# Block-diagonal inverse in an RWKV-7 scan: levels up to 32 on 64x64 blocks in four array positions, the mask applied to the first product

## What is computed

```python
def step(S, inp):                        # one head, state S is 64 x 64
    r_t, w_t, k_t, v_t, a_t, b_t = inp
    sa = jnp.einsum('bhij,bhj->bhi', S, a_t)
    S = (S * w_t[:, :, None, :]
         + sa[..., None] * b_t[:, :, None, :]
         + v_t[..., None] * k_t[:, :, None, :])
    y = jnp.einsum('bhij,bhj->bhi', S, r_t)
    return S, y
...
_, y = lax.scan(step, S0, xs)            # 512 steps, 16 heads
```

## Time and profile before

| | |
|---|---|
| median of 3 runs | 3165.78 us (3161.58 to 3166.35) |
| profiled execution | 3160.55 us, of which the span is 3158.7 us |
| PE busy over the span | 97% |
| DVE, ACT, POOL busy | 63%, 40%, 25% |
| the eight groups of the scan | 243.7 to 629.4 us from the span's start |

### The profile page before, as it was taken

One profiled execution on the slowest core, in us unless ns is written; L12 is line 12 of the kernel. 1 busy time (PEld: TensorE's weight loads), 2 busy tenths in 40 slices (PEclk: granted clock), 3 DMA queues, 4 the chain that ended last, 5 costly groups with the idle time before them and its releaser, 6 DMA issues.

```text
span 3158.7 us, 43525 instructions
## 1 busy us (share of the span) xinstructions
PE 3058.2 (97%) x17249; PEld 2662.7 (84%) x17249; DVE 1998.6 (63%) x3594; ACT 1266.9 (40%) x2141; POOL 776.0 (25%) x515
## 2 busy tenths in 40 slices
PE   8999999989999999999999999999999999999999
PEld 6778888878888888888877778999999998888887
DVE  5586665663232464333357755988978877787878
ACT  6364443343232334232234632435445453333432
POOL 1000110100000020000002200686776754343432
PEclk9999999999999999999999999999999999999999
DMA  4313221233333323333232022588889899999997
GB/s 123 111 31 101 62 74 57 72 119 94 100 94 100 114 94 92 95 97 97 87 91 74 1 68 81 185 270 299 304 284 323 290 315 376 366 355 354 353 358 269
DMA packets 233355, 539.43 MB, mean 171 GB/s; under 512 B 24817, under 2 KB 91633, under 8 KB 231105
## 3 DMA queue, kind: packets, MB, share of 16 engines
q1 hardware_dynamic: 177280, 375.11, 36.5%
q0 software_dynamic: 37440, 136.36, 11.7%
q10 hardware_dynamic: 18432, 25.17, 2.2%
HBM read 484.11 MB, written 52.46 MB: 170 GB/s over the span
## 4 chain that ended last, share of the span: by engine, by line
PE 81%; DVE 8%; POOL 3%; DMA 3%; ACT 2%; issue 1%; SPq 0%; DVEq 0%; ACTq 0%
PE bank L382 23%; PE bank L2822 16%; PE bank L385 16%; PE bank L2391 11%; PE bank L2551 2%; POOL etl L2379 2%; PE bank L1113 2%; PE bank L1124 2%; DMA eu<-in_peer_u 2%; PE bank L1077 1%; PE bank L505 1%; PE bank L1063 1%; POOL taken L2416 1%; PE bank L797 1%; DVE acc L1312 1%
## 5 line engine op out<-in xcount | busy, mean ns | idle before, releaser
L332 DVE TENSOR_TENSOR wl<-raw,wh 128x1024 fp32r<-128x1024 f32 (+2 forms) x241 | 294.5, 1225 | 643.4 <-ACT wh L317 643.3
L317 ACT CAST wh<-raw 128x1024 fp32r<-128x1024 f32 (+2 forms) x241 | 249.6, 1038 | 656.9 <-PE bank L382 367.2
L2379 POOL TENSOR_TENSOR etl<-eu,eth 128x1024 fp32r<-128x1024 f32 x128 | 317.7, 2483 | 384.0 <-ACT eth L2375 383.0
L2391 PE MATMUL bank<-peerhh,eth 128*128 128x384 f32 x1024 | 348.5, 340 | 11.2 <-POOL etl L2379 10.6
L2391 PE MATMUL bank<-peerhl,eth 128*128 128x384 f32 x1024 | 343.0, 335 | 0.0
L2391 PE MATMUL bank<-peerhh,etl 128*128 128x384 f32 x1024 | 342.9, 335 | 0.0
L2822 PE MATMUL bank<-vsh,coefh 128*128 128x512 f32 x768 | 299.1, 389 | 1.9 <-DVE coefl L2887 1.8
L2822 PE MATMUL bank<-vsh,coefl 128*128 128x512 f32 x768 | 298.8, 389 | 0.0
L2822 PE MATMUL bank<-vsl,coefh 128*128 128x512 f32 x768 | 298.8, 389 | 0.0
L2416 POOL DMA_INDIRECT taken<-in_peer_v,gb x128 | 210.0, 1641 | 298.4 <-DVE y_row L2436 293.1
L2391 PEld LDWEIGHTS bank<-peerhh,eth 128*128 128x128 f32 x1024 | 192.9, 188 | 14.7 <-ACT eg L2399 8.6
(11 more groups left out here) (577 smaller groups left out, 7118.2 us busy)
## 6 DMA issues: line engine op xcount, KB each, us to landing
eu<-in_peer_u SPq DMA_DIRECT2D x128, 512.0 KB, 4.3
vb<-in_peer_v SPq DMA_DIRECT2D x128, 512.0 KB, 5.9
raw<-in_ada_w SPq DMA_DIRECT2D x48, 512.0 KB, 3.9
acts<-eg ACTq DMA_DIRECT2D x128, 192.0 KB, 4.3
coefs<-stage SPq DMA_DIRECT2D x24, 1024.0 KB, 10.2
gd<-coefs SPq DMA_DIRECT2D x16, 1536.0 KB, 10.9
gl<-acts SPq DMA_DIRECT2D x128, 192.0 KB, 7.2
raw<-in_ffn_w_gate SPq DMA_DIRECT2D x44, 512.0 KB, 3.7
```

The source lines that it names most:

```text
L317: act.copy(parts_of(c)[0], raw_of(c)).then_inc(*up("w rounded", c))
L332: dve.tensor_tensor(lo, raw_of(c), hi.bitcast(F32), ALU.subtract).then_inc(*up("w split", c))
L2379: pool.tensor_tensor(Et[j % 3][1], Eu[j % 2], Et[j % 3][0].bitcast(F32), ALU.subtract).then_inc(*up("u split", j))
L2391: t = pe.matmul(b, tb[un][:, k * 128:(k + 1) * 128], peer_h[hn][:, k, 1:4, :], start=k == 0 and i == 0, stop=k == 7 and i == 2)
```

## The change

The six levels of full matrices become five levels (`l` = 1 to 5) on the two 64 x 64 diagonal blocks of each head, and the last step (64 to 128) becomes two small products. Four heads make a half `w` of the group, so a level has two halves instead of four units.

- W is made of 64 x 64 products, two per head (`p` is the diagonal block), whose four combinations of rows and columns of the array alternate (`pe_level_w`).
- The mask is applied to W: DVE copies the new entries of W into a unit matrix kept for this level and half (`eyes`, 12 of them, prepared once by POOL). That matrix times X is then the whole new X, without a mask.
- X and its transpose are both made as products from XT and that matrix (`pe_level_x`), and ACT copies both. There are no transposes in the levels.
- After level 5, `low` is A's lower block times X and `corner` that times the other block: the off-diagonal block of the full inverse. DVE copies a part of the last XT (L1471 after).
- The first X comes from an own product `first` (`pe_first`) under the smallest mask; its transpose is `pe_first_turned`.
- PSUM is taken in pairs of banks (`take_pair`) for these.
- The grids move: AK after level 1, RB after level 3, RK after level 5. The ada pieces move: after levels 2, 4 and 5, and three behind the next group's AT grid.

```diff
-            for li in range(1, 7):
-                for u, (q, hv) in enumerate(UNITS):
-                    b, before = banks.take(("w", g, li, u), ("w copied", g, li, u))
...
-                    on_pe.wait_ge(*(at("x new", g, li - 1, u) if li > 1 else at("turned", g, 0, u)))
-                    for i in range(2):
-                        t = pe.matmul(b[:, i * 128:(i + 1) * 128], S_[q]["AT"][:, 2 * hv + i, :],
-                                      S_[q]["X"][:, 2 * hv + i, :], start=True, stop=True)
-                    t.then_inc(*up("w full", g, li, u))
...
-                if li < 6:
-                    for u in range(4):
-                        turn(g, li, u)
-                if li in TASKS:
-                    pe_grids(pe, on_pe, g, TASKS[li])
...
+            for l in range(1, 6):
+                for w in range(2):
+                    pe_level_w(pe, on_pe, g, l, w)
+                for w in range(2):
+                    pe_level_x(pe, on_pe, g, l, w)
+                if l in TASKS:
+                    pe_grids(pe, on_pe, g, TASKS[l])
+                if l in ADAS:
+                    total(6 * g + ADAS[l])
+            for w in range(2):
+                pe_low(pe, on_pe, g, w)
...
+    def pe_level_w(pe, on_pe, g, l, w):
+        b, before = banks.take_pair(("w", g, l, w), ("scan dve", "w new", g, l, w))
+        for what in before:
+            on_pe.wait_ge(*at(*what))
+        for q in range(2):
+            on_pe.wait_ge(*at("grid", g, "AT", q))
+        on_pe.wait_ge(*(at("scan act", "x new", g, l - 1, w) if l > 1 else at("scan dve", "x first", g, w)))
+        x, order = (part(Xc, w), SIDES[l - 1]) if l > 1 else (eye(0, w), SIDES[1])
+        for h in sorted(range(4), key=lambda h: spot(SIDES[l], h)[::-1]):
+            (bank, n), (q, i), c = spot(SIDES[l], h), head(w, h), spots(order, h)
+            for p in range(2):
+                t = pe.matmul(b[side(p ^ bank), bank, 64 * n:64 * n + 64], grids[q]["AT"][side(p), i, side(p)],
+                              x[side(p), c:c + 64], start=True, stop=True)
+        t.then_inc(*up("scan pe", "w full", g, l, w))
+
+    def pe_level_x(pe, on_pe, g, l, w):
...
+            for p in range(2 if l < 5 else 1):
+                at_ = side(p ^ SIDES[l][h])
+                t = pe.matmul(b[side(p), bank, 64 * n:64 * n + 64], part(XTc, w)[at_, c:c + 64],
+                              eye(l, w)[at_, cw:cw + 64], start=True, stop=True)
+        t.then_inc(*up("scan pe", "x full", g, l, w))
...
+            for l in range(1, 6):
+                for w in range(2):
+                    on_dve.wait_ge(*at("scan pe", "w full", g, l, w))
+                    dve.copy_predicated(four(eye(l, w)), small_mask(l), bank_four(banks.pair(("w", g, l, w)), 0)).then_inc(
+                        *up("scan dve", "w new", g, l, w))
```

More of the change, by code:

```diff
@@ L1052, in pe_grids @@
         l_, r__, _ = GRIDS[name]
[L1053 to L1056, removed]
+        b, before = banks.take_pair(("grid", g, name), ("grid", g, name, 0), ("grid", g, name, 1))
+        for what in before:
+            on_pe.wait_ge(*at(*what))
         c0 = g // 2 * 128
@@ new lines, in pe_low @@
+    def pe_low(pe, on_pe, g, w):
+        b, before = banks.take(("low bank", g, w), ("scan act", "low", g, w))
+        for what in before:
+            on_pe.wait_ge(*at(*what))
+        on_pe.wait_ge(*at("scan act", "x new", g, 5, w))
+        for h in range(4):
+            q, i = head(w, h)
+            t = pe.matmul(b[64:128, 64 * h:64 * h + 64], grids[q]["AT"][0:64, i, 64:128],
+                          part(Xc, w)[0:64, 64 * h:64 * h + 64], start=True, stop=True)
+        t.then_inc(*up("scan pe", "low full", g, w))
@@ new lines, in pe_corner @@
+    def pe_corner(pe, on_pe, g, w):
+        b, before = banks.take(("corner bank", g, w), ("scan act", "corner", g, w))
+        for what in before:
+            on_pe.wait_ge(*at(*what))
+        on_pe.wait_ge(*at("scan act", "low", g, w))
+        on_pe.wait_ge(*at("scan dve", "xt low", g, w))
+        for h in range(4):
+            q, i = head(w, h)
+            t = pe.matmul(b[0:64, 64 * h:64 * h + 64], part(Vc, w)[64:128, 64 * h:64 * h + 64],
+                          XTf[64:128, q, i, 64:128], start=True, stop=True)
+        t.then_inc(*up("scan pe", "corner full", g, w))
@@ L1155, in pe_scan @@
             on_pe.wait_ge(*at("g copied", g))
[L1156 to L1157 removed]
+            for w in range(2):
+                on_pe.wait_ge(*at("scan act", "xt new", g, 5, w))
+                on_pe.wait_ge(*at("scan dve", "xt low", g, w))
+                on_pe.wait_ge(*at("scan act", "corner", g, w))
             for i, pf in enumerate(pairs(g)):
@@ L1283, in dve_first @@
             dve_grid(dve, on_dve, g, "AT", q)
-            on_dve.wait_ge(*at("xt eye", g, q))
-            on_dve.wait_ge(*at("grid", g, "AT", q))
-            dve.copy_predicated(sets[g][q]["XT"], mk(M1T), sets[g][q]["AT"]).then_inc(*up("xt first", g, q))
+        on_dve.wait_ge(*at("scan pe", "first full", g))
+        on_dve.wait_ge(*at("eyes"))
+        for w in range(2):
+            dve.copy_predicated(four(eye(0, w)), small_mask(0), bank_four(banks.pair(("first", g)), 128 * w)).then_inc(
+                *up("scan dve", "x first", g, w))
     def dve_scan(dve, on_dve):
```

284 lines of the change are left out of this document (170 added, 114 removed).

## The result

The median of four runs is 3112.3 us (3106.77 to 3125.62) against 3165.31 us (3161.58 to 3166.35) for the kernel before. The ratio is 0.9841, with a 95% interval of 0.9824 to 0.9857 (the two medians alone give 0.9832): 53 us less, where 76 were predicted. The execution with the profile took 3106.77 us and has a span of 3105.0.

A forecast was written before the change was run, and what follows sets the result against it. PE was taken to bound the kernel, with DVE at 62%. The layout's 94 us less, minus 18 us for the clock, left 76 off 3165.8: 3090 us, own range 3065 to 3110, 8 in 10 within 3045 to 3128.

The forecast's parts named there:

- the clock stays low: Rival: the clock is low through the scan's levels, 46 us back instead of 18, giving 3118 us; chance 0.14.
- A half product at 0.26 us: PE in the levels: 16 passes of one half product take 0.26 us, priced by columns per position; range 0.23 to 0.35.
- a price per pass: Rival: PE pays per pass, so a half product takes 0.51 us, giving 3126 us; chance 0.10.
- positions don't run at once: Rival: the four array positions run singly, 64 ns per pass, giving 3200 us; chance 0.04.
- The waits of the layout: Timed middle group: PE waits for DVE's masked copies, 1.4 us at level 2, 4.2 before level 5, 7.4 in all.
- The layout's wait at level 3 behind the ada piece: Level 3 of a group: masked copies wait for DVE's ada piece and run from 6.9 to 7.8 us.
- fewer waits: Rival: DVE's queue hides more, half the layout's 7.4 us of waits and no clock loss, giving 3042 us; chance 0.14.
- The layout's sum: Scan, all eight groups: middle groups fall from 50.2 to 38.4 us, together 94 us less.
- The clock takes some back: Scan: 6.8 us per group at the low clock after idle PE costs 2.3 us per group, 18 us in all.
- The bounds (0 and 46): Clock loss in the scan: none, or 46 us if levels 1 to 5 and one tail stretch run low.
- The start: covered: Before the scan: POOL writes unit matrices in 9.6 us, until 231.5; PE's first transposes stay within 1 us of 235.9.
- Behind the scan the same times: After the scan: times as before, shifted as a whole.

The follow-up runs named there:

- 6: Changed kernel with the products of a half issued position by position instead of alternating over the four array positions; 3113.01 us.
- 1: Changed kernel plus 16 unused 128x128 products on PE between W and X of level 5, in groups 1 to 7; 3084.74 us.
- 7: Kernel 4 (RB and RK grids behind levels 2 and 3) plus 16 unused products behind W of level 5; 3108.06 us.
- 4: Changed kernel with the RB and RK grids put back behind levels 2 and 3; 3165.59 us, ratio 1.0005 to the kernel before.
- 3: Changed kernel with ada loads, except the first column group's, cut to 16 of 128 partitions (modulation vector not the reference's); 3098.71 us.
- 8: Changed kernel with ada loads, except the first column group's, cut to one of 128 partitions (modulation vector not the reference's); 3111.32 us.
- 10: Changed kernel with the group norm split as in 2 and all ada pieces moved out of the levels, no unused products; 3064.67 us.
- 5: Kernel 2 plus 5, 5, 2 and 7 unused products behind W of levels 2 to 5; 3073.09 us.
- 2: Changed kernel with the group norm split: centre and square after level 2, scale and root after level 4; 3085.51 us.
- 9: Kernel 10 plus 5, 5, 2 and 2 unused products behind W of levels 2 to 5; 3079.19 us.

## Why the prediction was right, and where its size was off

The sign and the range of 8 in 10 held: 3090 predicted, 3112.3 measured, within 3045 to 3128. The narrower range of the forecast itself, 3065 to 3110, was missed by 2 us, and the number lies nearer to the 3118 of the rival *the clock stays low* than to the forecast. Of the 22 us that are missing between the spans, some 18 are the clock, 2 the layout, and 2 the start and what stands behind the scan. Point by point:

- **A half product at 0.26 us: right.** Starts lie 0.23 to 0.26 us apart. The rival *a price per pass* (0.51) fell with the first rows of the timeline, and *positions don't run at once* with it: passes at one position start 0.058 us apart, near the 0.064 that it took, and those at four positions in a quarter of that. 6 adds that not even their order matters. The prediction set beside this a rule of the Trainium skill (page "TensorE: Matmul & The Clock Gate", section on 56 against 53.3 ns), that matmuls never start closer than some 25 ns. Here 16 passes start within 0.23 to 0.26 us, 14 to 16 ns each on average, so the measurement decides against it for products at four positions.
- **The waits of the layout: right in place and size, but for one.** 1.4 us behind the copies of AK and of RB, 3.95 to 4.65 at level 5 (1.4 and 4.2 predicted), 7.1 us per group in all (7.4 in the layout). The layout's wait at level 3 behind the ada piece isn't among them. DVE's copies behind a grid took 1.33 us for two, as taken, and DVE was busy for 22.5 to 24.5 us in a middle group (25 predicted). Middle groups took 36.5 to 53.7 us, where 39 to 42 were named; their clock lies between 0.68 and 0.96. The rival *fewer waits* fell. The Trainium skill says (page "TensorEngine Tiling (Array Packing)", section on the PSUM bottleneck) that tiling speeds up TensorE and not the copies out of PSUM. This trace agrees in part: PE waits 56.8 us for masked copies out of PSUM, but in 30.4 of them the copy stands behind the group norm, which isn't such a copy.
- **The layout's sum: right within what can be told.** At 0.4 us for each low one (0.36 to 0.42 in 1, 6 and 7, 0.37 within kernels) the scan of the changed kernel at full clock is 329.8 - 0.4 x 99 = 290 us, and that of before 385.7 - 0.4 x 8 = 382.5. The layout's groups summed to 292, and its gain was 94; by this estimate it is 92. The issue waits, 8.5 us, are in the 290, so the rest went up to 10 us faster than laid out. It is less where an issue wait covers one for a copy: in group 5 one of 1.51 us stands where the other groups wait 1.4 us behind RB's copies.
- **"The clock takes some back": the term that was mis-sized.** It took 6.8 us at the low level per group and 18 us for the scan. Measured are 99 us at the low level, 12.4 per group, and 0.4 x 99 less before's 0.4 x 8, about 36 us back. The bounds (0 and 46) held it. The price was near, a third of a microsecond for each against 0.37 to 0.4; the low time was 54 us where 99 came. Two things were wrong in it. I extrapolated from one idle time to one stretch after it, while stretches of 20.5 and 34.1 us occur, and the longer one runs on through the tail, with PE busy in 33.29 of 34.1 us. And I counted on the idle time before level 5 alone; 4 shows that where the grids stand among the levels weighs as much. So the case that came true lies between my forecast and the rival *the clock stays low*, 0.85 where I said 0.9 and 0.8.
- **What the prediction lacked: issue waits**, 8.5 us in the changed kernel, 7.3 and 7.8 in 3 and 8, and from 2.5 (7) to 11.8 (1) in the others. Their cause stays open. They are in every kernel with the small products that was run and not in the scan of before. PE has 2560 more passes now (19809 against 17249), and the queue that brings instructions moved 2.57 MB instead of 2.24. That PE runs through its instructions faster than they are brought would fit this, but isn't shown.
- **The start: covered, as said, but late for another reason.** POOL wrote the unit matrices in 6.68 us (9.6 predicted), until 228.6, and was done with its memsets at 233.1. The first transposes start at 238.13, 2.3 us after those of before, not within 1 us: PE, busy throughout, ran at the low level from 230.50 to 237.30; before, the mean was 0.71 from 230.50 to 236.40. The scan itself began only 0.6 us later.

```profile
230.50:237.30 6.80, 6.80 (x9) 2.43 (x8) 0.69 (x1) 0.48 (x1) 2.63 (x4) 0.50 0.01 2
```

- **Behind the scan the same times**: within 1.6 us over 2530.

The clock as cause, and not as a companion of the waits, is shown by 1 and 7: they add only unused work in idle time and gain 27.6 and 57.5 us. A fill also takes a bank of the ring, which shifts the banks behind it. But executions of one and the same kernel, with the same banks, give 0.37 us for each low one, and 1 and 7 come to 0.38 by the medians, so nothing is left over for the banks. That the clock accounts for 36 of the 92 us is an estimate from these prices; the profiled scans of 8 and the changed kernel come to 0.57 for each low one, so the price isn't a constant. What makes the clock fall, beyond that filled idle time keeps it up, and what ends a low stretch stay open too.

## What to carry to other kernels

When a change makes PE's work light, price what the clock does over the whole stage and not over the one idle time behind it: here it took back about 36 of 92 us, and the placing of two grids among the levels decided over all of the gain. Read the granted clock group by group, since a mean over the stage hides a group at 0.68 beside one at 0.96, and of several executions, since one kernel's differ by up to 34 us with it (6). To keep it up, first move other engines' work out of the waits (10, some 100 us under before). Unused products in idle time paid where much low time was left, in long waits (1 and 7) and in short ones (5 against 2, 12.4 us); where little was left they cost more than they brought (9 against 10, 14.5 us). So measure them.

## What the runs showed of the hardware that was not expected

- Sixteen 64 x 64 passes of 64 columns at four array positions take 0.23 to 0.26 us, 14 to 16 ns each on average, whether the positions alternate or come one after another (6). At one position each takes 58 ns.
- PE can stay at the low level for 34.1 us while it is busy for 33.29 of them.
- The same kernel spends more or less time at the low level from one execution to the next, and each microsecond of it goes with 0.37 us of time.
- Sixteen unused products per group, put into idle time, took 27.6 us off one kernel and 57.5 off another.
- The kernels with many small passes have waits of PE on issue of up to 2.8 us at a time, with 88 GB/s of DMA as with 18.
